# Block one in the order u, z, gates, a, glu, wb, wa, wo, with x rewritten in normed form behind u

## The reference, cut to what matters

```python
h = rmsnorm(x, norm_g)                     # x * rsqrt(mean(x*x)) * g
v, bg, cg, za, u, zb, ga, gb = split(h @ w_in)
ya = bg * causal_depthwise_conv(cg * v, conv_w)
ya = (ya * silu(za)) @ w_out_a
yb = gelu(s5_scan(u, ...))                 # 64 groups, 64 states
yb = yb * sigmoid(yb @ w_glu + b_glu)
yb = (yb * silu(zb)) @ w_out_b
m = sigmoid(ga) * ya + sigmoid(gb) * yb
x = rmsnorm(x + m @ w_o, final_g)
```

## Time and profile before

| | |
|---|---|
| runs | 2502.61, 2502.80, 2502.87 us |
| span of the profiled execution | 2501.5 us; the page gives no other time for it, so 1.3 us of the median lie outside |
| TensorE busy | 2491.3 us in 11932 matmuls, 100% |
| VectorE, ScalarE, GpSimd busy | 1660.5, 848.8, 383.1 us |
| TensorE's share of the chain that ended last | 99% |
| moved between DRAM and SBUF | 353.07 MB, mean 141 GB/s |
| granted clock of TensorE | 0.999 over the span |

### The profile page before, as it was taken

One profiled execution on the slowest core, in us unless ns is written; L12 is line 12 of the kernel. 1 busy time (PEld: TensorE's weight loads), 2 busy tenths in 40 slices (PEclk: granted clock), 3 DMA queues, 4 the chain that ended last, 5 costly groups with the idle time before them and its releaser, 6 DMA issues.

```text
span 2501.5 us, 30081 instructions
## 1 busy us (share of the span) xinstructions
PE 2491.3 (100%) x11932; PEld 2157.3 (86%) x11932; DVE 1660.5 (66%) x2218; ACT 848.8 (34%) x1153; POOL 383.1 (15%) x286
## 2 busy tenths in 40 slices
PE   9999999999999999999999999999999999999998
PEld 8888888888888888888888888878888888888888
DVE  7789888998988776555554885657566564244434
ACT  5222222222222322223322333333565664333432
POOL 0045343444443431000000000000000000000001
PEclk9999999999999999999999999999999999999999
DMA  5333333333333433667666676624322222322333
GB/s 202 103 121 111 119 120 115 122 117 111 119 111 128 136 123 126 218 222 253 204 209 212 211 249 211 218 91 152 101 85 85 85 77 93 118 96 92 124 127 126
DMA packets 117963, 353.07 MB, mean 141 GB/s; under 512 B 15424, under 2 KB 18752, under 8 KB 117824
## 3 DMA queue, kind: packets, MB, share of 16 engines
q1 hardware_dynamic: 117824, 351.16, 42.4%
HBM read 321.68 MB, written 23.07 MB: 138 GB/s over the span
## 4 chain that ended last, share of the span: by engine, by line
PE 99%; DVE 0%; DMA 0%; SPq 0%; ACT 0%; issue 0%; DVEq 0%
PE bank L552 29%; PE bank L553 29%; PE bank L554 29%; PE bank L752 2%; PE bank L753 2%; PE bank L751 2%; PE bank L805 1%; PE bank L795 1%; PE bank L615 1%; PE bank L603 1%; PE bank L715 1%; PE bank L788 0%; PE bank L786 0%; DMA W<-in_w 0%; PE bank L847 0%; PE bank L767 0%
## 5 line engine op out<-in xcount | busy, mean ns | idle before, releaser
L1273 DVE TENSOR_TENSOR WL<-W,WH 128x1024 fp32r<-128x1024 f32 (+1 forms) x452 | 600.9, 1333 | 441.1 <-ACT WH L924 440.1
L924 ACT ACTIVATE WH<-W 128x1024 fp32r<-128x1024 f32 (+1 forms) x452 | 473.8, 1050 | 900.5 <-PE bank L554 653.4
L552 PE MATMUL bank<-hH,WH 128*128 128x512 f32 x1792 | 681.3, 380 | 0.8 <-DVE hL L1569 0.3
L554 PE MATMUL bank<-hH,WL 128*128 128x512 f32 x1792 | 679.3, 379 | 0.0
L553 PE MATMUL bank<-hL,WH 128*128 128x512 f32 x1792 | 679.3, 379 | 0.0
L552 PEld LDWEIGHTS bank<-hH,WH 128*128 128x128 f32 x1792 | 338.7, 189 | 58.2 <-issue 5.0
L554 PEld LDWEIGHTS bank<-hH,WL 128*128 128x128 f32 x1792 | 338.7, 189 | 48.1
L553 PEld LDWEIGHTS bank<-hL,WH 128*128 128x128 f32 x1792 | 338.9, 189 | 47.2
L552 PE MATMUL bank<-h2H,WH 128*128 128x512 f32 x624 | 239.4, 384 | 0.0
L553 PE MATMUL bank<-h2L,WH 128*128 128x512 f32 x624 | 236.6, 379 | 0.0
L554 PE MATMUL bank<-h2H,WL 128*128 128x512 f32 x624 | 236.6, 379 | 0.0
(11 more groups left out here) (308 smaller groups left out, 3608.9 us busy)
## 6 DMA issues: line engine op xcount, KB each, us to landing
W<-in_w SPq DMA_DIRECT2D x332, 512.0 KB, 3.7
W<-in_ada SPq DMA_DIRECT2D x96, 512.0 KB, 4.3
W<-in_wa SPq DMA_DIRECT2D x32, 512.0 KB, 3.9
W<-in_wo SPq DMA_DIRECT2D x32, 512.0 KB, 3.8
W<-in_wvv SPq DMA_DIRECT2D x32, 512.0 KB, 3.7
W<-in_wb SPq DMA_DIRECT2D x16, 512.0 KB, 3.7
URAW<-U SPq DMA_DIRECT2D x96, 64.0 KB, 3.1
scr_am<-SO SPq DMA_DIRECT2D x16, 256.0 KB, 2.0
```

The lines of the kernel that those rows point to most:

```text
L552: e.matmul(o, wh, xh, start=first, stop=False)
L554: return e.matmul(o, wl, xh, start=False, stop=last)
L924: e.activation(chunk_parts(n)[0][:, c], W[:, i % NW, c], ACT.Copy).then_inc(sem["hi"], 1)
L1273: e.tensor_tensor(wl[:, c], W[:, plan.item_of[n] % NW, c], wh[:, c].bitcast(F32), ALU.subtract).then_inc(sem["lo_v"], 1)
```

## The change

Block one's order becomes u (0 to 15), z (16 to 31), gates (32 to 95), a (96 to 223), glu (224 to 231), wb (232 to 247), wa (248 to 279), wo (280 to 311). Block two's order stays.

- **x rewritten.** Once `RSA` is there, GpSimd multiplies the 16 groups of x by it in place. ScalarE rewrites `hH` and VectorE `hL` from that (`normed`): groups 0 to 7 when TensorE is done with chunk 14, groups 8 to 15 when it is done with chunk 15. z's first projection waits for each group (`n_ready`). The products with `RSA` behind z, gates and a are gone, and ScalarE reads those banks itself.
- **State space.** Tiles spread over the chunks 28 to 199 (`SSM_C`: until a's thirteenth channel group), and wait for the last rewritten group of x, whose place they take. Two products of the parameters use `T` as scratch instead of `V`.
- **a's product** comes back beside glu and wb (`AM_AT`) and is split there; y's gelu and parts are made beside a's last channel group. wb's result waits in `MB` and wa's joins it, instead of the other way round.
- **Adaptive sums.** Twelve stand in every second chunk of glu and wb, 52 in each chunk of wa and the first 20 of wo. The last two parts (32 chunks) move to block two, chunks 392 to 421, with two of them at once at chunks 392 and 407; counted from 0, part 4's sums and part 5's first two products thus come in VectorE's turn of chunk 406, ahead of the layer norm.

```diff
-SSM_GATES = 13
+SSM_C = 12
...
-A_GATES = 16
 ADA_ORDER = (2, 3, 0, 1, 4, 5)
+AM_AT = {1: 0, 3: 1, 5: 2, 7: 3, 8: 4, 9: 5, 10: 6, 12: 7, 13: 8, 14: 9, 16: 10, 17: 11, 18: 12, 20: 13, 21: 14,
+         22: 15}
...
+        for m in range(8):
+            self.proj("zb", [w1[72 + m, c] for c in range(2)])
+        for m in range(32):
+            self.proj("gate", [w1[80 + m, c] for c in range(2)])
         for c in range(16):
             for part in (0, 2, 1, 3):
                 self.proj("a", [w1[16 * part + c, kc] for kc in range(2)])
-        for m in range(8):
-            self.proj("zb", [w1[72 + m, c] for c in range(2)])
-        for m in range(32):
-            if m == SSM_GATES + 1:
-                self.ada = [t["ada"][part, k] if k < 16 else None for part in ADA_ORDER for k in range(20)]
-            self.proj("gate", [w1[80 + m, c] for c in range(2)])
-        for m in range(16):
-            self.proj("wa", [t["wa"][m, c] for c in range(2)])
+        ada = [t["ada"][part, k] for part in ADA_ORDER for k in range(16)]
+        for i in range(12):
+            self.ada += [ada[i:i + 1], []]
+        self.ada += [[x] for x in ada[12:64]]
         for m in range(8):
             self.proj("wg", [t["wg"][m, 0]])
         for m in range(16):
             self.proj("wb", [t["wb"][m, 0]])
+        for m in range(16):
+            self.proj("wa", [t["wa"][m, c] for c in range(2)])
...
+        for i in range(0, 32, 16):
+            self.ada += [[], []] if i == 0 else []
+            self.ada += [ada[64 + i:66 + i]] + [[x] for x in ada[66 + i:80 + i]]
...
-    MA = at("MA", 0, [128, 16, 512])
-    ybH, ybL = at("ybH", 32, [128, 8, 512], F32R), at("ybL", 48, [128, 8, 512], F32R)
-    mL = at("mL", 32, [128, 16, 512], F32R)
+    mL = at("mL", 64, [128, 16, 512], F32R)
...
-    AH, AL = at("AH", 64, [128, 16, 512], F32R), at("AL", 96, [128, 16, 512], F32R)
+    AH, AL = at("AH", 0, [128, 16, 512], F32R), at("AL", 32, [128, 16, 512], F32R)
...
-    ACC = at("ACC", 198.25, [128, 1024])
+    ACC = [at("ACC0", 198.25, [128, 1024]), at("ACC1", 24, [128, 1024])]
...
-    tiles_to = plan.last(gate_p[SSM_GATES - 1])
+    tiles_to = plan.last(a_p[4 * SSM_C + 3])
...
-            e.wait_ge(*nth("xl", 15))
-            e.wait_ge(*nth("xacc", 15))
+            e.wait_ge(*nth("xl", 31))
...
+        def load_a(at):
+
+            k = AM_AT.get(at)
+            if k is not None:
+                if k >= 2:
+                    e.wait_ge(*nth("al_v", k - 2))
+                e.dma_start(SO[:, k % 2, :], scratch["am"][k]).then_inc(am_in[k % 2], 16)
+
+        for g in range(8):
+            if g >= 2:
+                e.wait_ge(*nth("g_v", g - 2, 2))
+            load(scratch["zb"][g])
+            load_a(g)
+            unit()
...
+        def n_ready(k):
+            e.wait_ge(*nth("xl", 16 + k))
+
+        for i, p in enumerate(spill_p + a_p):
+            project(p, xh, xl, n_ready if i == 0 else None, beside=ssm_until)
...
+        def normed(k):
+            e.wait_ge(sem["used"], plan.last(u_p[7]) + k // 8)
+            e.wait_ge(*nth("xn", k))
+            e.activation(hH[:, k, :], XS[:, k, :], ACT.Identity, scale=col["g1"][:, k:k + 1]).then_inc(sem["xh"], 1)
+
+        for k in range(8):
+            normed(k)
+        for s, p in enumerate(spill_p):
+            ssm_until(unit())
+            if s == 0:
+                for k in range(8, 16):
+                    normed(k)
+            ssm_until(unit())
+            projected(p)
+            if s >= 2:
+                e.wait_ge(spilled[s % 2], 16 * (s // 2))
+            e.activation(halves(SO[:, s % 2, :]), tokens(bank[bank_of[p]][:, :]),
+                         ACT.Silu if s < 8 else ACT.Sigmoid).then_inc(sem["sp_a"], 1)
...
+        def gelu_y(i):
+            if i == 0:
+                e.wait_ge(*nth("skip", 7))
+            e.activation(U[:, i, :], U[:, i, :], ACT.Gelu_apprx_tanh).then_inc(sem["yb_a"], 1)
+
+        def high_y(i):
+            e.wait_ge(sem["yb_a"], i + 1)
+            e.activation(ybH[:, i, :], U[:, i, :], ACT.Copy).then_inc(sem["yb_a"], 1)
...
+                if c == 15:
+                    for k in range(4 * (i % 2), 4 * (i % 2) + 4):
+                        (gelu_y if i < 2 else high_y)(k)
...
+                if i == 3:
+                    projected(p)
+                    if c > 0:
+                        e.wait_ge(*nth("a_v", c - 1, 6))
+                    e.activation(halves(T[:, 2, :]), tokens(bank[bank_of[p]][:, :]), ACT.Silu).then_inc(sem["a_a"], 1)
...
+        def high_a(at):
+            k = AM_AT.get(at)
+            if k is not None:
+                e.wait_ge(am_in[k % 2], 16 * (k // 2 + 1))
+                e.activation(AH[:, k, :], SO[:, k % 2, :], ACT.Copy).then_inc(sem["al_a"], 1)
...
-            t3, t4 = (V[:, i, :].rearrange("p (j c) -> p j c", c=16) for i in range(2))
+            t3, t4 = (T[:, i, :].rearrange("p (j c) -> p j c", c=16) for i in range(2))
             frb = fr.unsqueeze(2).to_broadcast([128, 32, 16])
             fib = fi.unsqueeze(2).to_broadcast([128, 32, 16])
-            e.wait_ge(*nth("xl", 15))
-            e.wait_ge(*nth("xsq", 15))
+            e.wait_ge(*nth("xacc", 15))
...
-        e.tensor_tensor(RSS, RSA[:, :], RSA[:, :], ALU.mult).then_inc(sem["rss"], 1)
-        e.memset(CV[:, 0:2], 0.0).then_inc(sem["rss"], 1)
-        e.wait_ge(sem["rss"], 2)
+        def normed(k):
+            e.wait_ge(*nth("xh", 16 + k))
+            e.scalar_tensor_tensor(out=hL[:, k, :], in0=XS[:, k, :], scalar=col["g1"][:, k:k + 1],
+                                   in1=hH[:, k, :].bitcast(F32), op0=ALU.mult,
+                                   op1=ALU.subtract).then_inc(sem["xl"], 1)
+
+        for k in range(8):
+            normed(k)
+        for s in range(len(spill_p)):
+            ssm_until(unit())
...
-                    e.tensor_tensor(cv, cv, RSS, ALU.mult).then_inc(sem["a_v"], 1)
...
-        for s, p in enumerate(spill_p):
-            for _ in range(2):
-                ssm_until(unit())
-            c = s - 8 - A_GATES
-            if c >= 0:
-                e.wait_ge(*nth("al_a", c))
-                e.tensor_tensor(AL[:, c, :], SI[:, c % 2, :], AH[:, c, :].bitcast(F32),
-                                ALU.subtract).then_inc(sem["al_v"], 1)
-            projected(p)
-            e.wait_ge(spilled[s % 2], 16 * (s // 2 + 8))
-            e.tensor_tensor(halves(SO[:, s % 2, :]), tokens(bank[bank_of[p]][:, :]), halves(RSA[:, :]),
-                            ALU.mult).then_inc(sem["sp_v"], 1)
...
+        def low_a(at):
+            k = AM_AT.get(at)
+            if k is not None:
+                e.wait_ge(*nth("al_a", k))
+                e.tensor_tensor(AL[:, k, :], SO[:, k % 2, :], AH[:, k, :].bitcast(F32),
+                                ALU.subtract).then_inc(sem["al_v"], 1)
...
-            e.memset(CB[:, :, :, :], 0.0).then_inc(sem["cb0"], 1)
...
+        e.memset(CB[:, :, :, :], 0.0).then_inc(sem["cb0"], 1)
+        e.wait_ge(*nth("rsa", 0))
+        for k in range(16):
+            e.wait_ge(*nth("xsq", k))
+            e.wait_ge(*nth("xl", k))
+            e.tensor_tensor(XS[:, k, :], XS[:, k, :], RSA[:, :], ALU.mult).then_inc(sem["xn"], 1)
...
-            e.wait_ge(*nth("a_a", c, 2))
-            e.wait_ge(*nth("rsa", 0))
-            e.tensor_tensor(T[:, 2, :], T[:, 2, :], RSA[:, :], ALU.mult).then_inc(sem["a_p"], 1)
...
```

213 lines of the change are left out of this document (91 added, 122 removed).

## The result

The changed kernel takes 2515.7 us (median of four runs, 2515.0 to 2516.8) against 2502.8, a ratio of 1.0052 with an interval of 1.0038 to 1.0066: 12.9 us slower, where 8.5 was forecast and 2515.5 the upper end of the range. The profiled execution has a span of 2515.6 us, 14.1 more than before; at 2516.8 us it is the slowest of the four, so about one of the 14.1 is not in the median.

A forecast was written before the change was run, and what follows sets the result against it. The prediction took TensorE to bound the kernel from 24.4 us to the end. To the median of 2502.8 us it added 6.2 and 2.3 us of waits, giving 2511.3 us, with an 8-in-10 range of 2508.0 to 2515.5 us.

The forecast's parts named there:

- TensorE sets the time, the change can only open waits: Whole kernel: TensorE is the chain from 24.4 us to the end, so nothing is won there.
- What is removed costs nothing: VectorE and GpSimd products beside TensorE: their removal, the moved sums and the copies of a all put at nothing.
- First term: Chunks 16 and 17: normed low parts of x come late in VectorE's queue; 6.2 us together, bounds 0 and 7.6.
- Nor does GpSimd ... 15 us of spare time hold even if each takes twice as long: GpSimd's 16 products from 53.1 us end at 74, first wanted at 89.8, so they do not set the first term.
- Pauses of 3.2 and 2.8 us, as here, would leave it alone: TensorE's clock after the pauses at chunks 16 and 17: stays at 2.4 GHz, no slow matmuls.
- The quiet end of the kernel: Tail, 2494 to 2499 us: 2.4 GHz held for at least four quiet microseconds, taken as evidence against a slow clock.
- rival 2: Clock falls at the second pause, around chunk 17: 2.0 us more, 2513.3 us; chance 0.10.
- Second term: Block two's gate projections: adaptive sums ahead of the layer norm delay low parts of weights; 2.3 us, bounds 0 and 5.
- the single steps of 0.3, 0.4, 0.6 and 1.0: Four TensorE waits for low parts of weights in block two's gate projections, in us, making up the 2.3 us.

The follow-up runs named there:

- z0_noprod: The changed kernel without GpSimd's 16 products of x, so the factor 1/rms is left out of z, gates and a: 2511.13 us.
- c2_chain_order: The changed kernel with GpSimd's products waiting for one another, normed low parts ahead of parameter work, part 5's sums on chunks 416-422 and 426-434: 2508.38 us.
- z1_late: The changed kernel with the 21 parameter phases on chunks 4 to 36 and the tiles from chunk 40: 2514.47 us.
- c3_chain_order_late: c2_chain_order with the 21 parameter phases on chunks 4 to 36 and the tiles from chunk 40: 2503.68 us.
- y4_pool_same: The kernel before plus 16 unread GpSimd products of x by the spread factor from 53 us, without waits but one after the eighth: 2506.68 us.
- x3_sums: The changed kernel with part 4's sums two chunks earlier and part 5's moved to chunks 416 to 431, none beside the layer norm: 2516.32 us.

## Why the prediction was wrong, step by step

- **TensorE sets the time, the change can only open waits:** right. The whole difference is pauses and slow matmuls behind them.
- **What is removed costs nothing, nor do the moved sums and copies of block one:** right. There is no new wait in z, gates, a, glu, wb or wa behind chunk 18, and VectorE has less to do there, where it was looked at (64 of 100 us busy from 200 to 300, before 89).
- **First term, 3.2 + 2.8 (with the rounding, 6.2):** right in mechanism and size. z0_noprod has 3.2 and 2.9 at the forecast places, the changed kernel 3.2 and 2.9 from a start 4.5 us late. Its stated cause, the place in VectorE's queue behind other work, is part of it, and the amount of that work is the other part. With the order changed and TensorE not yet late, 1.5 and 1.3 are left (c2_chain_order); with the load spread and the old order, 1.8 and 1.3 (z1_late); with both, none (c3_chain_order_late).
- **"Nor does GpSimd ... 15 us of spare time hold even if each takes twice as long":** this step failed. It asked when GpSimd would be done, and was right about that; it did not ask what VectorE would do meanwhile. The products made VectorE's short operations over six times as long, 2.8 us of pause at chunk 12. y4_pool_same shows it in the kernel before. The Trainium skill ("SBUF — State Buffer", Who interferes with whom) has the rule: VectorE and GpSimd share a pair of ports, one holds it for a whole instruction and the other stands, while an operation of VectorE with at most one source in SBUF and outside the two-port modes goes on. The traces agree (1.2 us against 0.17 for operations on SM, 0.62 each for the reads of a bank), and by this rule the rows of before would have given a rival: up to 16 stands of 1.28 us in VectorE's queue of 53 to 74 us.
- **"Pauses of 3.2 and 2.8 us, as here, would leave it alone":** this failed too. The quiet end of the kernel is one sample, and the runs show that pauses of about three microseconds go either way. The clock halved twice, 1.8 us each, of which rival 2 had one, at 2.0. Its remark that a slow stretch behind the first pause is hidden by the second is what z0_noprod shows. The Trainium skill ("TensorE: Matmul & The Clock Gate", Part 1: The HAM clock gate) says that the period in which activity is counted runs freely beside the kernel; equal pauses with unequal ends agree with that, and no experiment here moved a pause against that period.
- **Second term, 2.3 us:** 1.8 measured; the sums as its cause are shown by x3_sums, where these waits are gone; the single steps of 0.3, 0.4, 0.6 and 1.0 came as 0.0, 0.3, 0.2 and 1.1. In c2_chain_order, with the sums elsewhere, the stretch costs 0.4 us, which is one moved reduction.
- **The sum:** 6.2 + 2.3 = 8.5 forecast; 2.8 + 1.8 + 1.8 missing, 0.1 too much in the first term and 0.5 in the second, 0.2 given back by the small matmuls: 14.1, as the two spans. Both missing pieces push upward, so the range, built from the bounds of the terms that were there, missed by 0.2 us. That it came so near is luck: it left room above for errors in the second term, and 6.4 us came from two terms that its sum put at nothing.
